# Attention scores and values on the whole TensorE array: zero-filled keys by parity of heads, forget sums as extra contraction rows

## The reference, cut to what matters

```
# first block, per head:  q (256, 64), k (256, 64), v (256, 64)
s = q @ k.T * SCALE                       # SCALE = 64 ** -0.5
p = softmax(where(key <= query, s, -inf));  y = p @ v

# second block, per head, with c = cumsum(log_sigmoid(f + bias)) over tokens
s = q @ k.T * SCALE
s = s + c[:, None] - c[None, :]           # the row term c[:, None] drops out of the softmax
p = softmax(where(key <= query, s, -inf));  y = p @ v
```

## Time and profile before

| | |
|---|---|
| median of 3 runs | 1196.91 us (1196.55 to 1197.66) |
| span of the profiled execution | 1196.8 us |
| PE busy | 1148.5 us, 96% |
| DVE busy | 481.1 us, 40% |
| ACT busy | 410.5 us, 34% |
| POOL busy | 222.0 us, 19% |
| HBM traffic | 330.9 MB, mean 277 GB/s |
| mean granted TensorE clock | 0.989 of full |

### The profile page before, as it was taken

One profiled execution on the slowest core, in us unless ns is written; L12 is line 12 of the kernel. 1 busy time (PEld: TensorE's weight loads), 2 busy tenths in 40 slices (PEclk: granted clock), 3 DMA queues, 4 the chain that ended last, 5 costly groups with the idle time before them and its releaser, 6 DMA issues.

```text
span 1196.8 us, 15588 instructions
## 1 busy us (share of the span) xinstructions
PE 1148.5 (96%) x5930; PEld 761.6 (64%) x5930; DVE 481.1 (40%) x971; ACT 410.5 (34%) x609; POOL 222.0 (19%) x100
## 2 busy tenths in 40 slices
PE   4999999999999999999989998999999999999998
PEld 2678867774444444444434435978877788888886
DVE  3475552753222222222212215589454653323226
ACT  3533454232111111111111115664245363444334
POOL 0163333300000000000000002200313444443522
PEclk8899999999999999999999998999999999999999
DMA  9897366689899999999999996453223464645541
GB/s 355 322 329 264 128 229 246 269 329 367 339 377 421 423 422 421 422 422 422 422 420 421 422 421 240 160 192 126 86 71 141 150 194 159 210 147 181 201 163 48
DMA packets 92329, 331.68 MB, mean 277 GB/s; under 512 B 3937, under 2 KB 26754, under 8 KB 66674
## 3 DMA queue, kind: packets, MB, share of 16 engines
q1 hardware_dynamic: 91648, 330.36, 71.2%
q0 software_dynamic: 432, 0.48, 0.2%
q10 hardware_dynamic: 194, 0.06, 0.0%
HBM read 329.84 MB, written 1.05 MB: 276 GB/s over the span
## 4 chain that ended last, share of the span: by engine, by line
PE 73%; DMA 16%; DVE 6%; issue 2%; ACT 2%; SPq 0%; DVEq 0%; ACTq 0%
DMA ring<-in_w 15%; PE ps L839 14%; PE ps L840 13%; PE ps L841 13%; PE ps L1196 13%; PE ps L1238 5%; PE ps L1168 1%; PE ps L1169 1%; DVE ring_r L1992 1%; PE ps L912 1%; DMA ring<-in_w_ada 1%; ACT ring_r L1550 1%; PE ps L1349 1%; PE ps L976 1%; PE ps L974 1%
## 5 line engine op out<-in xcount | busy, mean ns | idle before, releaser
L814 POOL TENSOR_TENSOR ring_r<-ring,ring_r 128x1024 fp32r<-128x1024 f32 x76 | 197.8, 2623 | 824.5 <-ACT ring_r L1550 824.4
L1196 PE MATMUL ps<-ring,arena 128*64 128x512 f32 x1008 | 226.0, 596 | 8.8 <-DMA ring<-in_w 7.7
L840 PE MATMUL ps<-ring_r,hl_r 128*128 128x512 f32 x528 | 211.4, 400 | 0.0
L839 PE MATMUL ps<-ring_r,hl_r 128*128 128x512 f32 x480 | 197.5, 411 | 10.7 <-DVE hr_r L2085 6.1
L841 PE MATMUL ps<-ring_r,hr_r 128*128 128x512 f32 x480 | 192.0, 400 | 0.0
L1550 ACT ACTIVATE ring_r<-ring 128x2048 fp32r<-128x2048 f32 x90 | 167.4, 1907 | 62.5 <-PE ps L841 45.0
L1196 PEld LDWEIGHTS ps<-ring,arena 128*64 128x64 f32 x1008 | 69.5, 137 | 149.0 <-issue 127.6
L1992 DVE TENSOR_TENSOR ring_r<-ring,ring_r 128x2048 fp32r<-128x2048 f32 x52 | 121.3, 2339 | 84.5 <-ACT ring_r L1550 84.3
L839 PEld LDWEIGHTS ps<-ring_r,hl_r 128*128 128x128 f32 x480 | 91.8, 191 | 41.2 <-issue 14.7
L840 PEld LDWEIGHTS ps<-ring_r,hl_r 128*128 128x128 f32 x528 | 101.0, 191 | 21.9
L841 PEld LDWEIGHTS ps<-ring_r,hr_r 128*128 128x128 f32 x480 | 91.8, 191 | 22.3
(11 more groups left out here) (370 smaller groups left out, 1650.7 us busy)
## 6 DMA issues: line engine op xcount, KB each, us to landing
ring<-in_w SPq DMA_DIRECT2D x91, 2048.0 KB, 21.5
ring<-in_w_in SPq DMA_DIRECT2D x21, 2048.0 KB, 8.4
ring<-in_w_ada SPq DMA_DIRECT2D x16, 1024.0 KB, 10.2
ring<-in_w_ffn_gate SPq DMA_DIRECT2D x11, 1024.0 KB, 5.2
ring<-in_w_ffn_up SPq DMA_DIRECT2D x11, 1024.0 KB, 7.8
ring<-in_w_ffn_down SPq DMA_DIRECT2D x5, 2048.0 KB, 7.8
ring<-in_w_ada SPq DMA_DIRECT2D x4, 2048.0 KB, 8.7
ring<-in_w_o SPq DMA_DIRECT2D x2, 2048.0 KB, 7.7
```

Source lines behind the costliest of these rows:

```text
L814: nc.gpsimd.tensor_tensor(rest[:, a:b], w[:, a:b], lead[:, a:b].bitcast(F32), ALU.subtract).then_inc(sem("w_rest_b"), 1)
L839: mm(o, lhsT=a_lead, rhs=b_lead, start=start, stop=False, skip_group_check=True)
L840: mm(o, lhsT=a_lead, rhs=b_rest, start=False, stop=False, skip_group_check=True)
L1196: last = mm(H[slots_of(e), :], lhsT=xs[:, k, slots_of(e)], rhs=w, start=k == 0, stop=k == KD - 1)
```

## The change

In the first block the keys are kept in two buffers, `kT[0]` for even heads and `kT[1]` for odd ones (this lies where `krow` was). Each has the head's keys on its 64 partitions and zeros on the other 64, which POOL writes. `scores` then takes all 128 partitions of `qT`, that is both heads' queries, against the buffer of its head's parity. In the second block queries too are kept by parity (`qT2[0]`, and `qT2[1]` where `qrow` was): on the other 64 partitions POOL writes columns of the identity, a one on partition j for the heads of tile j, and the same partitions of `kT` get the forget sums of the four heads of that parity. So the forget term comes out of the same contraction, and the per-head matmuls for it are gone. `forget_rows` makes these sums once for all heads (three matmuls, unit `foxc` in the small rotation), from a table `forget` that DVE builds. `by_parity` on ACT copies the four halves of 64 partitions where `copy_out` copied two tiles. `weighted_values` takes the 128 columns of `vrow` of two heads as the stationary operand and fills 128 partitions of PSUM, of which the readers take the head's 64, as before. `KE[0]` moves to the gates buffer. The semaphore counts follow.

```diff
--- before.py
+++ after.py
@@ arena and recurrence buffers
-        kT = part(16, 4).rearrange("p (c t) -> p c t", t=T)
+        kT = [part(at, 4).rearrange("p (c t) -> p c t", t=T) for at in (16, 4)]
+        qT2 = [part(at, 4).rearrange("p (c t) -> p c t", t=T) for at in (12, 0)]
+        forget = acc[:, 1, 0:2 * P].rearrange("p (t n) -> p t n", t=TT)
...
-        KE = [part(0, 4).rearrange("p (h t) -> p h t", t=T),
+        KE = [G16[:, 8:12, :],
...
-                small_order += ["tk_b0", "tk_b1"]
+                small_order += ["tk_b0", "tk_b1", "foxc"]
@@ POOL
+            nc.gpsimd.memset(kT[0][DH:P, :, :], 0.0).then_inc(sem("other_halves"), 1)
...
+                if m == M["cg"]:
+                    small.ready(pool, "tk1")
+                    pool.wait_ge(sem("w_rest_b"), rest_pool[m + 1])
+                    nc.gpsimd.memset(kT[1][0:DH, :, :], 0.0).then_inc(sem("other_halves"), 1)
...
+                if m == M["hq"]:
+                    pool.wait_ge(sem("w_rest_b"), rest_pool[m + 1])
+                    nc.gpsimd.tensor_copy(qT2[0][DH:P, :, :], ident[DH:P, DH:DH + 4].unsqueeze(2).to_broadcast(
+                        [DH, 4, T])).then_inc(sem("other_halves"), 1)
+                    small.ready(pool, "tq_b1")
+                    pool.wait_ge(sem("other_halves"), 3)
+                    nc.gpsimd.tensor_copy(qT2[1][0:DH, :, :], ident[0:DH, 0:4].unsqueeze(2).to_broadcast(
+                        [DH, 4, T])).then_inc(sem("other_halves"), 1)
@@ PE, scores
-                    for n, (t, s) in enumerate(((0, 0), (1, 0), (1, 1))):
-                        into = o[:, n * P:(n + 1) * P]
-                        mm(into, lhsT=qT[a:a + DH, h // 2, t * P:(t + 1) * P], rhs=kT[a:a + DH, h // 2, s * P:(s + 1) * P],
-                           start=True, stop=False)
-                        mm(into, lhsT=first, rhs=ones if s else upto, start=False, stop=s == 0)
-                    mm(o[:, 2 * P:SC], lhsT=second, rhs=upto, start=False, stop=True).then_inc(small.done, 1)
-                    return
-                mm(o[:, 0:P], lhsT=qT[a:a + DH, h // 2, 0:P], rhs=kT[a:a + DH, h // 2, 0:P], start=True, stop=True)
-                mm(o[:, P:SC], lhsT=qT[a:a + DH, h // 2, P:T], rhs=kT[a:a + DH, h // 2, :], start=True,
-                   stop=True).then_inc(small.done, 1)
+                    q = qT2[odd][:, h // 2, :]
+                else:
+                    q = qT[:, h // 2, :]
+                k = kT[odd][:, h // 2, :]
+                mm(o[:, 0:P], lhsT=q[:, 0:P], rhs=k[:, 0:P], start=True, stop=True)
+                mm(o[:, P:SC], lhsT=q[:, P:T], rhs=k, start=True, stop=True).then_inc(small.done, 1)
+
+            def forget_rows():
+                o = small.claim(pe, "foxc")
+                pe.wait_ge(sem("fox_c_ready"), 2)
+                mm(o[:, 0:P], lhsT=forget[:, 0, :], rhs=upto, start=True, stop=True)
+                mm(o[:, P:T], lhsT=forget[:, 0, :], rhs=ones, start=True, stop=False)
+                mm(o[:, P:T], lhsT=forget[:, 1, :], rhs=upto, start=False, stop=True).then_inc(small.done, 1)
@@ PE, weighted_values
-                mm(o[a:a + DH, 0:P], lhsT=vrow[:, 0, h * DH:(h + 1) * DH], rhs=p[:, 0:P], start=True, stop=True)
+                p, both = pT[:, h % 2, :], slice(h // 2 * P, (h // 2 + 1) * P)
+                mm(o[:, 0:P], lhsT=vrow[:, 0, both], rhs=p[:, 0:P], start=True, stop=True)
@@ ACT
+            def by_parity(name, tiles, ready):
+                for i in range(2):
+                    for odd in range(2):
+                        small.ready(act_, f"{name}{max(i, odd)}")
+                        src = small.bank(f"{name}{i}")
+                        rows = slice(odd * DH, (odd + 1) * DH)
+                        af(two_tiles(tiles[odd], i)[rows], src[rows, :].rearrange("p (c t) -> p c t", t=T),
+                           ACT.Copy).then_inc(sem(ready), 1)
...
-                    for i in range(2):
-                        copy_out(two_tiles(kT, i), small, f"tk_b{i}", "kT_ready")
+                    by_parity("tk_b", kT, "kT_ready")
+                    src = small.ready(act_, "foxc")
+                    for odd, rows in ((0, slice(DH, P)), (1, slice(0, DH))):
+                        af(kT[odd][rows], src[rows, 0:T].unsqueeze(1).to_broadcast([DH, 4, T]),
+                           ACT.Copy).then_inc(sem("kT_ready"), 1)
@@ DVE
-            v.tensor_scalar(fz[:, 0, :], fz[:, 0, :], -1.0 / SCALE, None, ALU.mult).then_inc(sem("fox_c_ready"), 1)
+            link(v.memset(forget, 0.0))
+            for odd in range(2):
+                v.tensor_scalar(forget[:, :, DH * (1 - odd):DH * (1 - odd) + 4],
+                                fz[:, 0, :].rearrange("p (t i two) -> p t i two", t=TT, two=2)[:, :, :, odd], -1.0 / SCALE, None,
+                                ALU.mult).then_inc(sem("fox_c_ready"), 1)
```

More of the change, by code:

```diff
@@ L432, in two_blocks @@
             small_released[f"yt{u}"] = sem("hy_rest"), u + 1
+            small_released[f"tq{u}"] = sem("qT_ready"), u + 1
+            small_released[f"tq_b{u}"] = sem("qT_ready"), 2 + 2 * u + 2
             for tag in ("", "_b"):
-                small_released[f"tq{tag}{u}"] = sem("qT_ready"), u + 1 + 2 * SECOND[tag]
-                small_released[f"tk{tag}{u}"] = sem("kT_ready"), u + 1 + 2 * SECOND[tag]
+                small_released[f"tk{tag}{u}"] = sem("kT_ready"), 2 * u + 2 + 4 * SECOND[tag]
+        small_released["foxc"] = sem("kT_ready"), 10
         for n, group in enumerate(("g2", "g3")):
@@ L965, in scores @@
                 o = small.claim(pe, f"qk{tag}{h}")
-                pe.wait_ge(sem("qT_ready"), h // 4 + 1 + 2 * SECOND[tag])
-                pe.wait_ge(sem("kT_ready"), h // 4 + 1 + 2 * SECOND[tag])
-                a = DH * (h % 2)
+                u, odd = h // 4, h % 2
+                pe.wait_ge(sem("other_halves"), odd + 1 + 2 * SECOND[tag])
                 if SECOND[tag]:
-                    pe.wait_ge(sem("fox_c_ready"), 1)
-                    first, second = (fz[:, 0, t * HEADS + h:t * HEADS + h + 1].to_broadcast([P, P]) for t in range(TT))
-                    for n, (t, s) in enumerate(((0, 0), (1, 0), (1, 1))):
-                        into = o[:, n * P:(n + 1) * P]
-                        mm(into, lhsT=qT[a:a + DH, h // 2, t * P:(t + 1) * P], rhs=kT[a:a + DH, h // 2, s * P:(s + 1) * P],
-                           start=True, stop=False)
-                        mm(into, lhsT=first, rhs=ones if s else upto, start=False, stop=s == 0)
-                    mm(o[:, 2 * P:SC], lhsT=second, rhs=upto, start=False, stop=True).then_inc(small.done, 1)
-                    return
@@ L1397, in _ @@
                     head_transposes("tk_b", krow, "k_normed", 2)
+                    forget_rows()
                 if name == "gate_b11":
@@ L1651, in _ @@
                     af(gates[:, u, n * COL:(n + 1) * COL], src, ACT.Tanh, scale=0.5).then_inc(sem("gates_ready"), 1)
-                if unit in ("xb0", "xb1"):
-                    which, dst = ("tq", qT) if unit == "xb0" else ("tk", kT)
+                if unit == "xb0":
                     for i in range(2):
-                        copy_out(two_tiles(dst, i), small, f"{which}{i}", f"{which[1]}T_ready")
+                        copy_out(two_tiles(qT, i), small, f"tq{i}", "qT_ready")
+                if unit == "xb1":
+                    by_parity("tk", kT, "kT_ready")
                 if unit in ATT1_AT:
@@ L1796, in _ @@
                 if unit == "fk1":
-                    for i in range(2):
-                        copy_out(two_tiles(qT, i), small, f"tq_b{i}", "qT_ready")
+                    by_parity("tq_b", qT2, "qT_ready")
                     decay(0)
```

13 lines of the change are left out of this document (9 added, 4 removed).

## The result

The kernel after takes 1184.9 us (median; 1183.7 to 1185.7) beside 1196.7 of the kernel before on the same chip: ratio 0.9894, 95% interval 0.9882 to 0.9905. A second series on another chip gave 0.9893 (0.9872 to 0.9914). It is faster by 11.8 us; 17.3 were forecast. The profiled execution has 1183.4 us against 1196.8, so 13.4 less.

What follows compares the result with a forecast made beforehand. PE's instruction stream was taken to bound attention, with DMA deciding in the experts. First block 5.9 us plus second block 13.2 (19.8 less 6.6 of waits) less 1.8 of additions gave 17.3, so 1179.6 us from 1196.9; range 1172 to 1188.5.

Steps and rivals of the forecast that it cites:

- more waits: Rival: POOL beside DVE in attention and one clock fall cost 3 to 6 us more, 1183 to 1186; chance 0.12.
- 256-column pair: Attention scores: the 256-column fp32 matmul pair takes 0.24 us, priced from fp32r rows; over 0.3 us would show it wrong.
- First block, 5.9 us: First block's attention on PE: full-array matmuls cut a full step from 2.22 to 1.45 us, 5.9 us in sum.
- That it passes the experts in full: Experts, where DMA decides: the whole train of weight transfers starts 5.9 us earlier, so all of that gain reaches the end.
- The rival with 0.10: Experts: transfers bound that stage, so the first block's gain is lost, 1185.5 us; chance 0.10.
- Second block, 19.8 us on PE: Second block's attention on PE: scores 18.1 us less, transposes 0.6, values 1.1, in sum 19.8 before new waits.
- The two long waits: Second block's attention: PE newly waits for DVE 3.1 us at step 4 (head 2's transposes) and 2.1 at step 7 (head 5's).
- The short ones, 1.4 in four places: Second block's attention: waits where ACT's weight copies stand ahead of exps or the copy of probabilities, 1.4 us in four places.
- The clock after a wait: Second block, within the more waits rival: the clock falls once after the 3 us wait, slowing eight dense matmuls, 1.6 us.
- Additions, 1.8 us: Work added ahead of second-block attention: forget_rows 0.7 us on PE, DVE chain 0.4, POOL's copy beside DVE 0.7; sum 1.8.
- Slower: Rival: the clock falls at step 4 of second-block attention and stays low through pa_b, 1202 us; chance 0.05.
- A 128-row matmul costs what the tiled one does: Rival: half-zero 128-row fp32 matmuls are no faster; block one gives 0, second block's scores 14.2 us, 1189; chance 0.05.

Runs made afterwards that it cites:

- e1: Kernel after with scores and values of the first block alone on half the array again; ratio to before 0.9942 (0.9921 to 0.9963).
- e5: Kernel after with DVE's normalise of head 2 of the second block moved ahead of hgrn_rows; ratio to before 0.9903 (0.9880 to 0.9925).
- second profile of after: Profile from running the kernel after once more, nothing changed; ratio to before 0.9893 (0.9872 to 0.9914).
- e9: Kernel after with second-block DVE work around hgrn reordered, yrow transposes one step later, POOL's second copy put off, forget memset on POOL; ratio to before 0.9852.
- e2: Kernel after with second-block scores as before (64-row halves, four forget sums a head), new tiles and forget_rows kept; 1194.2 us, ratio to before 0.9974.
- e6: Kernel after with DVE's values_rest of head 3 of the second block ahead of hgrn_rests; 1181.6 us in a single run.

## Why the prediction was right, and where its sizes were off

The forecast, faster and inside the range, held, and the mechanisms were the ones named. The sum said 17.3; the runs gave 11.8 and 12.5. The time lies 5.3 us from the point forecast, where the rival "more waits" had put it (1183 to 1186), but only in part by that rival's means: the fall of the clock is one, and a matmul pair that was priced too low is another. Two of the prediction's own signs of being wrong came true, the 256-column pair at over 0.3 us (0.43) and a granted clock below 1.00 in attention (0.97 in 850 to 905 us).

- **The 256-column pair**: the term that was mis-sized. The step "those are fp32r; I take the same for fp32, since at 128 columns the rate is already about that" failed. An fp32 instruction takes 0.11 us for 128 columns and 0.217 for 256, so the pair takes 0.43, not 0.24. The two fp32r rows can't price it. Over 16 heads that is 3.2 us too much in the sum. The trace of before had a row that could: fp32 matmuls of 512 columns in the routing, twelve instructions in 5.40 us, so 0.45 us each (their starts lie 0.43 apart).

```profile
256.49 5.40 PE L1143 MATMUL ps<-x,cst 128*128 128x512 f32 x12
```

  The Trainium skill, Perfetto Trace Analysis, "Engine Utilization", gives the array's output rate and half of it for FP32_LOW_HIGH. If that is what each of the two instructions runs at, an estimate from it is 0.107 us for 128 columns and 0.213 for 256, and these rows agree.
- **First block, 5.9 us**: the step took 1.65 and not 1.45. With 0.2 less for eight heads the same sum gives 4.3; the profiles of after and before differ by about 4 before the experts, and the runs of e1 by 5.8 with a wide interval.
- **That it passes the experts in full**: right. The rival with 0.10 looked true in the first pair of profiles (3.76 us became 1.70), and the distance of 467.3 to 467.5 us whatever the start, in the profiles without a fall of the clock, refutes it.
- **Second block, 19.8 us on PE**: eight periods shrank from 6.86 to 4.46, so 19.2. Of the 1.6 us too much for the scores, 1.0 came back at the values, where the changes of form that vanish are worth more than I took (transposes and values 1.22 to 0.92 in a step that dense matmuls follow, 883.71 to 884.63).
- **The two long waits**: right in place and nearly in size, 2.9 for 3.1 and 2.7 for 2.1 (2.8 and 2.5 as the profile lists them). The prediction named score_max and normalise as what the transposes need, and e5 shows that moving normalise alone doesn't help. The short ones, 1.4 in four places, are 1.5 in the second profile of after and none in the first.
- **The clock after a wait** was in a rival with 1.6 us and belonged in the sum: in nine of the ten profiles with a long wait the clock falls behind one, and 1.5 to 1.7 us go with it (2.6 in e9). Waits and clock together are 7.3 and 8.8 us in the two profiles of after, where the sum had 6.6.
- **Additions, 1.8 us**: 1.9 by e2. POOL's copy cost 0.84, at 0.7 taken.
- **The other rivals.** "Slower", by a fall of the clock that lasts: it fell, but only for a few microseconds behind a wait. "A 128-row matmul costs what the tiled one does": its premise is true, and its sum isn't. Scores of the kernel before, in the step of the earlier trace rows:

```profile
888.14 0.49 PE L974 MATMUL ps<-arena 64*128 64x128 f32 x2
888.55 0.49 PE L976 MATMUL ps<-cst,fz 128*128 128x128 f32 x2
888.88 0.39 PE L977 MATMUL ps<-cst,fz 128*128 128x128 f32 x2
```

  The pair on 64 rows is followed after 0.41 us, the full-array pair L976 behind it after 0.33, and the full-array pair L977, with its own form on both sides, after 0.22 (889.10). The full-array pair ahead of these rows, between two tiled ones (start 887.72), takes 0.42 as well. So it isn't the half array that is slow but each change of form, some 0.2 us, half of it ahead of the change and half behind; the gap of 0.09 that the prediction read is one such half. A period of the second block lost six changes in the scores (1.2 us), two around the values (0.3) and four forget matmuls (0.88), together about the 2.40 measured. The prediction took its prices from distances that held the changes, which is why the sum held without this.

Put together for the profiles: 4.3 + 19.2 - 7.3 - 1.9 is 14.3; the experts' entry at the lower clock took 2.1 from that, and a fall at 730 to 790 us that before had and after didn't gave back about 1.5. That is 13.7, and 13.4 were measured. What stays open is why the clock falls at 260 us in one execution and not in another of the same program; no run was aimed at it.

## What to carry to other kernels

Price a matmul by its own type, its own number of columns and the form of its neighbours; a row of another type at the right size, or of the right type at another size, is not the same, and some stage far away usually has the right row. When a faster engine meets a queue that was in time before, list everything the waiting instruction needs, its PSUM bank too, and what stands ahead of each giver on its engine; here three of four repairs moved the wait before the last removed it. And judge a gain of a few microseconds by a stretch between two marks in several profiles, since one pair of profiles can lose half of it to the clock of a stage that the change doesn't touch.

## What the runs showed of the hardware

- Behind a wait of PE of 2 to 3.7 us in a dense stretch the clock fell to the lower of its two levels in nine of ten profiles, and 1.5 to 1.7 us went to it (2.6 in e9, at a granted clock of 0.77 in 870 to 885 us). In e6 it stayed at 1.00 behind a wait of 2.9. Where two long waits stand, it fell behind the first in two profiles and behind the second in four, in two profiles of the same program once so and once so.
- POOL's subtractions of 2.33 us hold DVE instructions with a single operand in SBUF: 0.28 and 0.35 became 2.33 each, and one on 128x2 elements took 1.77 (in after 1.82 at 880.58, which PE didn't see). values_rest and score_max, which read PSUM, were not held (in after values_rest takes 0.43 at 879.31, inside POOL's 877.64 to 882.37).
- fp32 streams 128 columns in 0.11 us an instruction and 256 in 0.217, with no gap between instructions of the same form, on 64 rows as on 128; a change between 128x128 and 64x128 or 128x64 forms costs 0.14 to 0.2, spread over the instruction ahead and the one behind.
- A transfer-bound stage passed an earlier start on in full: 467.3 to 467.5 us from its first matmul to the next stage's in five profiles, over starts that differ by 4 us.
